# Six projection units computed chunk by chunk while the conditioning weights land, in a two-layer diffusion step on one Trainium2 core

## The reference, cut to what matters

```
m = silu(cond) @ ada_w + ada_b          # cond: one vector per token group; 6 parts of 1024
shift, scale, gate, ... = split(m)
h = x * rsqrt(mean(x*x) + EPS) * g * (1 + scale) + shift
qa, ka, va, qb, f_fwd, f_bwd, ib, gb = split(h @ w_in)      # w_in: 1024 x 3328
```

## Time and profile before

| | us |
|---|---|
| median of 3 runs | 986.39 (984.5 to 987.72) |
| span of the profiled execution, first to last instruction | 983.9 |
| TensorE busy | 900.8 (92%) |
| VectorE busy | 406.7 (41%) |
| ScalarE busy | 289.7 (29%) |
| GpSimd busy | 263.1 (27%) |

### The profile page before, as it was taken

How to read it: one execution, slowest core, us unless ns; L and a number is a source line. 1 busy time by engine, 2 the same in 40 slices (tenths; PEclk the granted TensorE clock), 3 DMA queues, 4 the chain that set the end, 5 groups by cost and what they waited for, 6 DMA issues and landing times.

```text
span 983.9 us, 13906 instructions
## 1 busy us (share of the span) xinstructions
PE 900.8 (92%) x5729; PEld 578.3 (59%) x5729; DVE 406.7 (41%) x762; ACT 289.7 (29%) x537; POOL 263.1 (27%) x175
## 2 busy tenths in 40 slices
PE   3899999978797998998999989999999899989996
PEld 1688898755565985333333379888588743323332
DVE  1653665566635462222223463222625602222245
ACT  2632243332433243111111364121552521101112
POOL 0156353300003301233233306230360113333330
PEclk9999999998996997999999999999999889999998
DMA  9675335412424958999886543330449959999815
GB/s 379 261 257 214 129 135 204 149 44 89 171 91 145 419 177 322 403 378 401 299 313 230 186 163 129 129 130 1 174 179 417 364 187 377 403 362 380 294 64 202
DMA packets 41598, 230.08 MB, mean 234 GB/s; under 512 B 14112, under 2 KB 15168, under 8 KB 21824
## 3 DMA queue, kind: packets, MB, share of 16 engines
q1 hardware_dynamic: 22608, 189.80, 50.5%
q0 software_dynamic: 14528, 28.61, 8.1%
q10 hardware_dynamic: 4400, 10.77, 3.1%
HBM read 279.58 MB, written 19.81 MB: 304 GB/s over the span
## 4 chain that ended last, share of the span: by engine, by line
PE 75%; DVE 9%; DMA 9%; ACT 4%; issue 2%; POOL 1%; ACTq 0%; POOLq 0%; DVEq 0%
PE ps L2094 17%; PE ps L1723 8%; PE ps L2108 8%; PE ps L1725 8%; PE ps L1724 8%; PE ps L1694 4%; DMA Z<-experts_up,par 4%; PE ps L2119 2%; DMA att<-h_rows,par 2%; PE ps L1858 2%; DVE Z L1180 2%; DMA xT<-x_columns 1%; DVE Z L1059 1%; PE ps L1709 1%; PE ps L1715 1%
## 5 line engine op out<-in xcount | busy, mean ns | idle before, releaser
L547 POOL TENSOR_TENSOR wlo<-raw,whi 128x1024 fp32r<-128x1024 f32 x57 | 139.2, 2462 | 355.4 <-ACT whi L663 353.0
L2094 PE MATMUL ps<-Z,att 128*64 128x512 f32 x704 | 192.5, 605 | 6.3 <-DMA Z<-experts_up,par 6.3
L2094 PEld LDWEIGHTS ps<-Z,att 128*64 128x64 f32 x704 | 58.1, 139 | 100.6 <-issue 100.6
L1723 PE MATMUL ps<-hhi,whi 128*128 128x384 f32 x296 | 104.9, 354 | 6.7 <-DVE hlo L1295 3.0
L1724 PE MATMUL ps<-hlo,whi 128*128 128x384 f32 x296 | 101.0, 341 | 0.0
L1725 PE MATMUL ps<-hhi,wlo 128*128 128x384 f32 x296 | 100.9, 341 | 0.0
L1059 DVE TENSOR_TENSOR att<-att,ps 128x256 f32<-128x256 f32 x28 | 11.8, 421 | 190.4 <-ACT att L870 184.7
L663 ACT ACTIVATE whi<-raw 128x1024 fp32r<-128x1024 f32 x58 | 59.8, 1054 | 86.3 <-DMA raw<-weights 56.2
L2108 PE MATMUL ps<-raw,att 128*64 128x512 f32 x272 | 80.2, 598 | 0.0
L1723 PE MATMUL ps<-whi,hhi 128*128 128x256 f32 (+1 forms) x264 | 74.9, 284 | 2.4 <-DVE hlo L1570 1.7
L1724 PE MATMUL ps<-wlo,hhi 128*128 128x256 f32 (+1 forms) x264 | 73.7, 279 | 0.0
(11 more groups left out here) (332 smaller groups left out, 1487.0 us busy)
## 6 DMA issues: line engine op xcount, KB each, us to landing
raw<-weights SPq DMA_DIRECT2D x69, 1024.0 KB, 4.9
Z<-experts_up SPq DMA_DIRECT2D x26, 2048.0 KB, 10.8
raw<-experts_down SPq DMA_DIRECT2D x20, 1024.0 KB, 9.0
spare<-experts_up SPq DMA_DIRECT2D x6, 2048.0 KB, 12.1
Z<-weights SPq DMA_DIRECT2D x8, 1024.0 KB, 16.5
hf<-experts_down SPq DMA_DIRECT2D x6, 1024.0 KB, 9.1
spare<-experts_down SPq DMA_DIRECT2D x6, 1024.0 KB, 8.9
Z<-y_rows SPq DMA_DIRECT2D x12, 512.0 KB, 6.0
```

Source lines behind the costliest of these rows:

```text
L547: nc.gpsimd.tensor_tensor(unit_view(wlo, u), raw_unit(n, half), unit_view(whi, u).bitcast(F32), ALU.subtract)\
L1723: mm(out, ahi, bhi, start=start, stop=False)
L2094: last = mm(out, h[:, k, c:c + HALF], ring(BLOCK_AT[q, z])[:, k, :], start=(k == 0), stop=(k == KC - 1))
```

## The change

- The layout of the first 8 slots: slot n holds chunk n of the shift and chunk n of the scale, where it held 256 neighbouring columns.
- SyncE issues `x` in two halves first, then the slots in the order of `FETCH_FIRST`, with the first three "in" slots among the 8 `ada` slots.
- The sum of squares is 8 matmuls of ones with the squares; the square root and the reciprocal are taken of 128x384 elements in place of 128x3.
- A loop over the 8 slots: `ada`, copy, turn, modulation of one chunk, high and low part of that chunk, and for each chunk the products of units 0 to 5, which have six banks (`FIRST_BANK`). The warm-up matmuls are gone. Units 1, 3 and 5 get their low part on VectorE.
- `ADA_AFTER` and `ROWS_AFTER`: no `ada` slot after units 0 and 2, two after unit 4 and two after unit 10; the row copies move from behind units 3 and 7 to behind 5 and 9.

```diff
-ADA_AFTER = [1, 1, 1, 1, 1, 1, 1, 1, 0, 2, 1, 1, 1]
+ADA_AFTER = [0, 0, 2, 1, 1, 2, 1, 1, 0, 2, 1, 1, 1]
-ROWS_AFTER = {3: 4, 7: 5, 11: 6, 15: 7, 19: 8, 23: 9}
+ROWS_AFTER = {5: 4, 9: 5, 11: 6, 15: 7, 19: 8, 23: 9}
+FETCH_FIRST = [0, 8, 1, 2, 9, 3, 4, 10, 5, 6, 7]
...
+            sp.dma_start(xT[:, 0:4, :], A["x_columns"][:, 0:4, :]).then_inc(S("in_x"), 16)
+            sp.dma_start(xT[:, 4:KC, :], A["x_columns"][:, 4:KC, :]).then_inc(S("in_x_rest"), 16)
+            for n in FETCH_FIRST:
+                fetch(n)
+            static(FIRST + RAW, B_P1 - 6)
...
+            nc.scalar.activation(nmax[:, 0:1], pcol[:, 0, 0:1], ACT.Sqrt, scale=0.0, bias=EPS)
...
+            for n in range(KC):
+                square(0, n)
+            act.wait_ge(S("ssum_ready"), SSUM["first"])
+            nc.scalar.activation(sums, bank(4, TOK), ACT.Sqrt, scale=1.0 / D, bias=EPS).then_inc(S("std_ready"), 1)
+            for n in range(KC):
+                first_row(n)
+                if n in (0, 2, 4):
+                    hi(n)
+                    hi(n + 1)
+                first_chunk(n)
...
+            V.reciprocal(sums, sums).then_inc(S("rcol_ready"), 1)
+            dve.wait_ge(S("rcol_ready"), 1)
+            first_norm(0)
+            first_norm(1)
+            for n in range(KC):
+                first_rows(n)
+                if n + 2 < KC:
+                    first_norm(n + 2)
+                if n in (0, 2, 4):
+                    unit_low(n + 1)
+                first_low(n)
...
+            def first_products(k, u0):
+                pe.wait_ge(S("hlo_ready"), k + 1)
+                unit_ready(u0 + 1)
+                for u in (u0, u0 + 1):
...
+            for n in range(KC):
+                ada(1)
+                if n >= 3:
+                    first_products(n - 1, 0)
+                first_turn(n)
+                if n in (1, 2):
+                    first_products(n - 1, 0)
+                for k in range(3) if n == 3 else [n - 1] if n > 3 else []:
+                    first_products(k, 2)
+                for k in {5: (0, 1), 6: (2, 3), 7: (4, 5, 6)}.get(n, ()):
+                    first_products(k, 4)
+            for u in (0, 2, 4):
+                first_products(KC - 1, u)
```

More of the change, by code:

```diff
@@ L38 @@
 RAW = 3
-ADA_BANK = (7, 6, 5, 3)
+FIRST_BANK = (0, 1, 2, 3, 5, 6)
 UNITS = 6
@@ L749, in _ @@
             for q in range(N_IN):
-                b, slot, half = q % 3, IN_ORDER[q // 2], q % 2
-                done = S(f"pb_free{b}")
+                b, slot, half = FIRST_BANK[q] if q < UNITS else q % 3, IN_ORDER[q // 2], q % 2
+                done = S(f"pb_free{q % 3}")
                 act.wait_ge(S("unit_used"), q + 1)
@@ L1121, in scaled, with first_norm @@
                     mul(hfk[:, k, :], xT[:, k, :], rstd).then_inc(S("xr_ready"), 1)
[L1123 to L1129, removed]
-            def first_rows(k):
[L1133 to L1136, removed]
+            first_mod, first_bias = (t.rearrange("p (z k) g -> p z k g", z=2) for t in (mod[:, 0, 0:16, :], pcol[:, 1, 0:16].unsqueeze(2).broadcast_to([P, 16, 2])))
+            def first_norm(k):
+                mul(hfk[:, k, :], xT[:, k, :], sums)
+            def first_rows(k):
+                dve.wait_ge(S("modT_ready"), k + 1)
+                ins = V.tensor_tensor(first_mod[:, :, k, :], bank(4, 4, TOK + 4 * k).rearrange("p (z g) -> p z g", z=2),
+                                      first_bias[:, :, k, :], ALU.add)
+                if k >= KC - 2:
+                    ins.then_inc(S("mod_ready"), 1)
+                    dve.wait_ge(S("mod_ready"), k - KC + 3)
+                else:
+                    link(ins)
+                ins = V.tensor_scalar(amp[:, 0, k, :], mod[:, 0, SC1 + k, :], 1.0, pcol[:, 0, N1 + k:N1 + k + 1], ALU.add, ALU.mult)
+                if k % 2 == 0:
+                    ins.then_inc(S("hf_rows"), 1)
+                else:
+                    link(ins)
+                    for g, t0, t1 in GROUPS:
+                        ins = V.tensor_scalar(hfk[:, k, t0:t1], hfk[:, k, t0:t1], amp[:, 0, k, g:g + 1], mod[:, 0, SH1 + k, g:g + 1],
+                                              ALU.mult, ALU.add)
+                    ins.then_inc(S("hf_rows"), 1)
             def first_low(k):
@@ L1810, in spread, with first_turn @@
                 last.then_inc(S("rstd_ready"), 1)
-            pe.wait_ge(S("act_start"), 1)
[L1814 to L1823, removed]
+            def first_turn(n):
+                pe.wait_ge(S("adarow_ready"), n + 1)
+                for z in range(2):
+                    o = 256 * n + P * z
+                    last = mm(bank(4, 2, TOK + 4 * n + 2 * z), adarow[:, o:o + P], con[:, C_SUM:C_SUM + 2], start=True, stop=True)
+                last.then_inc(S("modT_ready"), 1)
+            def first_products(k, u0):
+                pe.wait_ge(S("hlo_ready"), k + 1)
+                unit_ready(u0 + 1)
+                for u in (u0, u0 + 1):
+                    wh, wl = unit_view(whi, u), unit_view(wlo, u)
+                    last = three(bank(FIRST_BANK[u], TOK), wh[:, k, :], wl[:, k, :], hhi[:, k, :], hlo[:, k, :], k == 0, k == KC - 1)
+                    if k == KC - 1:
+                        last.then_inc(S("unit_used"), 1)
+            pe.wait_ge(S("in_con"), 16)
+            for k in range(KC):
+                pe.wait_ge(S("sq_ready"), k + 1)
+                last = mm(bank(4, TOK), ones, hfk[:, k, :], start=(k == 0), stop=(k == KC - 1))
+            last.then_inc(S("ssum_ready"), 1)
+            pe.wait_ge(S("act_start"), 1)
+            for n in range(KC):
[11 more added lines that the diff above has]
+                first_products(KC - 1, u)
             pair_cols = lambda c, b: slice(TOK * c + P * b, TOK * c + P * b + P)
```

104 lines of the change are left out of this document (41 added, 63 removed).

## The result

The changed kernel takes 1002.08 us (median of 4 runs, 996.14 to 1002.9) against 985.61 us for the kernel before on the same chip: ratio 1.0155, 95% interval 1.0128 to 1.0182, so it is slower, clear of noise. The forecast was 996.6 us, with a range of 984.5 to 1004. The profiled execution took 1001.39 us, its span is 999.4 us, 15.5 more than before.

What follows compares the result with a forecast made beforehand. TensorE, busy 92% of the span, was taken as the bound; waits in and behind the six units put the mark +10.2 us later, so span 983.9 became 994.1 and the median 996.6 us, range 984.5 to 1004.

Steps and rivals of the forecast that it cites:

- the likeliest case: The main forecast for the whole kernel: median 996.6 us, spanning 992 to 1001, chance 0.42.
- The start: Stretch up to the first product of the units, forecast to start at 24.2 us.
- The six units: Units 0 to 5 in the start: 34.9 us of work plus 5.9 of waits, done at 65.0 us.
- T: The instant when the six units end, forecast at 65.0 us; about 69 before the change.
- the chain row copy, high part, GpSimd, VectorE: Chain to the low parts of chunks 2 and 4, forecast to make TensorE wait 3.2 and 2.7 us.
- Behind the six units: Stretch from T to the mark, where late slot fetches lose the gain; mark forecast at 110.2 us.
- both knots: TensorE's waits for row copies before the ada slots behind units 6 and 10, forecast 3.5 and 3.1 us.
- the mark: Instant when the first products of the recurrence begin, forecast at 110.2 us against 100.0 before.
- The rival built on it: Fetches in ring order: second of a pair lands after 6.3 us, mark 104.9, time 991.3 us; chance 0.13.
- The sum: Total shift at the mark, +10.2 us, carried to the end: span 983.9 to 994.1, median 996.6 us.
- the rival that had it: Half clock after each stall: +10.2 plus 4 to 7 us, so 1001 to 1004 us; chance 0.15.
- One for one to the end: Behind the mark TensorE is the bound again, so a shift there reaches the end in full.

Runs made afterwards that it cites:

- the experiment on the reciprocal: Changed kernel with the reciprocal taken of one column, the other 383 left out: 999.21 us, ratio 1.0125.
- the two experiments with earlier high parts: Changed kernel with high parts of units 2 to 5 one chunk earlier: 996.12 us; the same plus ten matmuls, earlier row copies and unit 14 last: 980.64 us.
- the ten matmuls: Changed kernel with ten matmuls on constants keeping TensorE busy in front of the second turning: 998.67 us, ratio 1.0103.
- Cutting the chain: Changed kernel with high parts of units 2 to 5 and low parts of units 3 and 5 one chunk earlier: 996.12 us, ratio 1.0088.
- With the row copies earlier: Changed kernel with the row copies behind units 4 and 8 instead of 5 and 9: 994.84 us, ratio 1.0068.
- repaired: Changed kernel with early high parts, ten matmuls before the second turning, row copies behind units 4 and 8, unit 14's high part last: 980.64 us, ratio 0.9944.
- the old start with the same repairs: Kernel before with the new ada order, row copies behind units 4 and 8, and unit 14's high part last: 983.57 us, ratio 0.9989.

## Why the prediction was right, and where its sizes were off

The direction and the waits behind it were right; the time came 5.5 us above the forecast and 1 us above the likeliest case (992 to 1001). In brackets stands what was forecast.

**The start** came nearly as worked out. The sum of squares began at 8.10 (8.5) and ended at 15.7 (15.8), the reciprocal took 2.55 (2.54), the first product began at 24.49 (24.2). A little luck is in the first: the parameters landed earlier and the squares began at 7.13 (8.0), but the weight load of the sum waited until 8.09 for the constants, a transfer that the forecast didn't have. The lock between VectorE and GpSimd is in it: the first two scalings took 2.50 beside GpSimd, and 1.03 in the experiment on the reciprocal, where they ended before it began. That is 1.5; the forecast's own terms (21.3 against 18.8 and two of 0.5) give 1.5 as well, where it says 1.7. And an operation of 0.23 took 2.19 beside GpSimd at 30.38, and the two experiments with earlier high parts moved it to chunk 1 without removing it. This fits what the Trainium skill (SBUF — State Buffer, Who interferes with whom) says of the shared port pair.

**The six units** is the term that was mis-sized. T was to be 65.0 and is 70.5. The waits were smaller than forecast (1.19 and 2.41 us for 3.2 and 2.7, and 0.5 in front of a turning), because TensorE was slower in front of them; the clock cost more. Windows give up to 7.9 us lost at half clock in the start, where I had one stretch of 1.8. 24.5 + 33.1 of work at full clock + 4.1 + 7.9 is 69.6; 0.9 is not accounted for. That this part was bound by the chain row copy, high part, GpSimd, VectorE, as the prediction said, three experiments show. With the short reciprocal and with the ten matmuls the first product comes 1.1 us earlier and the clock costs 2.5 and 3.1 us less up to 34.6 us, but the wait in front of chunk 2 grows by 1.65, half clock follows it, and only 1.0 and 1.4 are won at T. Cutting the chain wins 4.9.

**Behind the six units** both knots were where the prediction had them. From T to the `ada` behind unit 6 it is 10.8 us (forecast 12.0), the wait 3.29 (3.5); behind unit 10 1.75 (3.1); at the mark 3.69. Slots 15, 20 and 22 took 6.8, 7.9 and 6.4 us from issue to landing, where I took 7.9 for each. The Trainium skill (DMA: Bandwidth & Descriptors, Queues, rings and completion order) has a ring's descriptors consumed in order, which gave an estimate of 6.3: two of three lie near it, one at the older row. The rival built on it (991.3) still was wrong: the 1.1 to 1.5 us saved on a transfer were taken by the clock, 3.2 us lost behind the first knot. From T to the mark it is 44.5 us, forecast 45.2.

**The sum** was +10.2 at the mark and +15.03 came: 5.5 from T, -0.7 behind it. The price of half clock that the likeliest case left out is the difference, and the rival that had it (1001 to 1004, chance 0.15) holds the measured 1002.08; the range held because it took in most of that rival. The argument against it, that slower products in front of a transfer-bound wait only shorten the wait, held in the start before chunk 2 and failed behind the first knot, where TensorE ran 20 us before it waited again. The price isn't the same in every trace, though: none was paid behind the first knot in the experiment on the reciprocal (3.16 us of idling, then 1.00).

**One for one to the end**: ScalarE's instructions stand 15.0 us later at 205 us, 14.0 at 560 and 15.4 at the last. The high part of unit 14 put last in the kernel before shows that 1.5 us won up to 184 us can be lost at 200.

## What to carry to other kernels

When work is moved forward into a start, ask first which buffers its neighbours release and behind which instruction each waited copy stands: here about half of the loss was made by two lists that were moved along with it, and one place in ScalarE's queue was worth 7 to 8 us. Count for each new wait of TensorE a slower stretch behind it too, as a bound and not as a certainty (here behind 2.41, 3.29 and 3.69 us, not behind 1.11 and 1.75, and not behind 3.16 in another variant), unless a wait follows that absorbs it. And judge a restructured start only after its followers are repaired: as it was it cost 16 us, repaired it is 5 us better than the old kernel and about 3 better than the old start with the same repairs.

## What the hardware did that was not expected

- The stretch at half clock behind an idle one had no fixed length: about 9 us behind 4.84 us of idling, 6.8 behind 2.41 and 3.29, 3.4 behind 3.69. With the row copies earlier, the same wait of 2.41 us had 3.4 behind it; with the short reciprocal, 3.16 us had none. The same place in two kernels shows 1.00 and 0.57 at 40 to 44 us and 0.66 and 0.50 at 195 to 200, with no longer wait in front of either. This would explain much of the spread of 7 to 9 us between runs of one kernel; it wasn't tested.
- Two 1 MB fetches issued 0.86 us apart landed within 7.3 to 7.7 us of the first issue in the changed kernel, while those 1.3 us apart took 9.2 and 9.5 before. What sets the difference was not tried.
